# Feed-forward of a two-block transformer kernel: the order of a chunk's send and the fetch of the chunk before it

## The reference

```python
def swiglu(h, w_gu, w_down):
    gate, up = jnp.split(h @ w_gu, 2, axis=-1)
    return (jax.nn.silu(gate) * up) @ w_down

for i in range(DEPTH):                                   # 4
    x = x + 0.5 * swiglu(rmsnorm(x, ffn1_norm[i]), ffn1_w_gu[i], ffn1_w_down[i])
    ...                                                  # mixer of layer i
    x = x + 0.5 * swiglu(rmsnorm(x, ffn2_norm[i]), ffn2_w_gu[i], ffn2_w_down[i])
```

## Time and profile before

| | |
|---|---|
| median of three runs | 2867.24 us (2863.96 to 2867.93) |
| profiled execution | 2865.28 us, of which the span is 2863.5 us |
| TensorE busy in the span | 2830.5 us, 99% |
| VectorE, ScalarE, GpSimd busy | 69%, 57%, 16% |
| DMA, mean over the span | 212 GB/s |

### The profile page before, as it was taken

The page is one execution under the profiler, slowest core; times in us unless marked ns, Lnnn a source line. Parts: engine busy times, 40 slices in busy tenths (PEclk is TensorE's granted clock), DMA queues, the critical chain, the costliest instruction groups (busy, mean ns, idle before and its releaser), DMA issues. The chain is left out here.

```text
span 2863.5 us, 36218 instructions
## 1 busy us (share of the span) xinstructions
PE 2830.5 (99%) x14207; PEld 2400.4 (84%) x14207; DVE 1966.8 (69%) x2300; ACT 1636.1 (57%) x2030; POOL 444.8 (16%) x724
## 2 busy tenths in 40 slices
PE   9999999999999999999999999999999999999998
PEld 7889888888988888888888898878888888888887
DVE  6868578677667768567767686676675765665764
ACT  5547755555464555565555487654566563566562
POOL 0304412021002112041201116111000020000020
PEclk9999999999999999999999999999999999999999
DMA  8964279697559779537869753596645696645694
GB/s 265 304 201 142 87 215 297 208 275 242 177 155 273 242 230 292 190 130 238 278 211 290 216 159 104 166 282 220 203 148 176 216 287 215 190 154 177 215 284 148
DMA packets 430842, 608.48 MB, mean 212 GB/s; under 512 B 21040, under 2 KB 282416, under 8 KB 430672
## 3 DMA queue, kind: packets, MB, share of 16 engines
q1 hardware_dynamic: 406416, 542.18, 60.1%
q0 software_dynamic: 23680, 62.95, 7.2%
q10 hardware_dynamic: 576, 1.05, 0.1%
HBM read 573.58 MB, written 32.51 MB: 212 GB/s over the span
## 5 line engine op out<-in xcount | busy, mean ns | idle before, releaser
L824 ACT ACTIVATE hi<-raw 128x2048 fp32r<-128x2048 f32 (+2 forms) x511 | 950.1, 1870 | 684.1 <-DMA raw<-in_ffn_w_gu 210.1
L862 DVE TENSOR_TENSOR lo<-raw,hi 128x2048 fp32r<-128x2048 f32 (+2 forms) x497 | 1098.3, 2229 | 277.8 <-ACT hi L824 276.2
L476 PE MATMUL ps<-hi,xh 128*128 128x512 f32 (+1 forms) x1952 | 766.9, 393 | 1.0 <-DVE lo L862 1.0
L478 PE MATMUL ps<-hi,xl 128*128 128x512 f32 (+1 forms) x1952 | 759.6, 389 | 0.0
L477 PE MATMUL ps<-lo,xh 128*128 128x512 f32 (+1 forms) x1952 | 759.0, 389 | 0.0
L478 PEld LDWEIGHTS ps<-hi,xl 128*128 128x128 f32 x1952 | 367.1, 188 | 76.0
L476 PEld LDWEIGHTS ps<-hi,xh 128*128 128x128 f32 x1952 | 367.5, 188 | 74.9 <-DVE lo L862 1.4
L477 PEld LDWEIGHTS ps<-lo,xh 128*128 128x128 f32 x1952 | 367.4, 188 | 72.7
L476 PE MATMUL ps<-hi,hhh 128*128 128x512 f32 x704 | 274.9, 390 | 0.6 <-DVE hhb L1352 0.6
L477 PE MATMUL ps<-lo,hhh 128*128 128x512 f32 x704 | 274.0, 389 | 0.0
L478 PE MATMUL ps<-hi,hhl 128*128 128x512 f32 x704 | 274.0, 389 | 0.0
(11 more groups left out here) (466 smaller groups left out, 3876.3 us busy)
## 6 DMA issues: line engine op xcount, KB each, us to landing
raw<-in_ffn_w_gu SPq DMA_DIRECT2D x396, 512.0 KB, 5.2
raw<-in_ffn_w_down SPq DMA_DIRECT2D x80, 1024.0 KB, 5.7
raw<-in_w_ff SPq DMA_DIRECT2D x64, 1024.0 KB, 5.6
raw<-in_w_in SPq DMA_DIRECT2D x60, 1024.0 KB, 5.3
raw<-in_gdn_w_in SPq DMA_DIRECT2D x32, 1024.0 KB, 5.6
turned<-hhf POOLq DMA_DIRECT2D x88, 256.0 KB, 4.5
hhr<-turned POOLq DMA_DIRECT2D x352, 64.0 KB, 4.2
raw<-in_sb_w_in SPq DMA_DIRECT2D x12, 1024.0 KB, 5.1
```

Of the source, the lines that this page charges most:

```text
L476: e.matmul(o, a1, r1, start=kk == 0, stop=False)
L478: i = e.matmul(o, a2, r1, start=False, stop=kk == kts - 1)
L824: k.e.activation(plan.part(m.hi, m, q), plan.part(m.raw, m, q), ACT.Copy).then_inc(*k.up("act_piece_hi", ("hi", q)))
L862: k.e.tensor_tensor(plan.part(m.lo, m, q), plan.part(m.raw, m, q), plan.part(m.hi, m, q).bitcast(F32), ALU.subtract).then_inc(*k.up("dve_p ...
```

## The change

`pool_hidden` is cut into two helpers, `send` and `fetch`, with the same instructions and waits as before. In the eight feed-forwards of the first block the order is the old one up to chunk 6. From chunk 7 on, chunk c is sent ahead of the fetch of chunk c - 1: send 7, send 8, fetch 7, send 9, fetch 8, send 10, fetch 9, fetch 10. The feed-forward of the second block (`ff2`) keeps the old order throughout.

```diff
     n = f.n // 4
-    for c in range(f.chunks):
+
+    def send(c):
         k.wait_ge("flip", g, c)
         if c >= 4:
             k.wait_ge("fetched", g, c - 4)
         k.e.dma_start(k.t["turned"][c % 4, :, 0:f.n], f.flipped[c % f.turns][:, :]).then_inc(*k.up(f"dma_send{c % 3}", ("sent", g, c), by=16))
+
+    def fetch(c):
         k.wait_ge("sent", g, c)
         for b in range(4):
             rows = k.t["turned"][c % 4, :, n * b:n * b + n].rearrange("(a i) r -> i a r", a=4)
             k.e.dma_start(f.raw[32 * b:32 * b + 32, c + 1, :].rearrange("i (a r) -> i a r", a=4), rows).then_inc(
                 *k.up(f"dma_fetch{c % 3}", *([("fetched", g, c)] if b == 3 else []), by=16))
+
+    ahead = 7 if si.name != "ff2" else f.chunks
+    for c in range(f.chunks):
+        send(c)
+        if c < ahead:
+            fetch(c)
+        elif c > ahead:
+            fetch(c - 1)
+    if ahead < f.chunks:
+        fetch(f.chunks - 1)
```

## The result

The changed kernel takes 2877.4 us (median of five runs, 2870.46 to 2881.11) against 2867.24 (five runs, 2863.45 to 2869.8). The ratio is 1.0032 with a 95% interval of 1.0019 to 1.0045: slower by about 9 us, with an interval of 5.4 to 12.9 us, where 1.4 were forecast. A second set of runs of the same kernel gave 1.0033 (1.0020 to 1.0045).

A forecast was written before the change was run, and what follows sets the result against it. TensorE, busy 2830.5 of 2863.5 us, was taken to bound the kernel. In the first feed-forward 1.5 + 6.9 - 7.0 = 1.4 us of stall, added to the median 2867.24, gave 2868.6 us; range 2865.0 to 2873.5.

The forecast's parts named there:

- the delay d: First feed-forward: how much later the fetch of 7 lands for ScalarE's turn; taken as 1.5 us, ends -0.4 and 4.4.
- The weight piece: First feed-forward, third piece of the down projection, behind the turn of 7: cover 2.26 us, so no cost at d 1.5.
- d - 2.26: TensorE's cost in us at that weight piece: nothing at d 1.5, 1.2 at 3.4.
- The term of the sum, chunk 9: First feed-forward: the fetch of 9 waits for flip 10 and the send of 10, stalling TensorE at chunk 10 by 1.4 us.
- d + L - 7.0: TensorE's stall at chunk 10 where positive; L, landing of the fetch of 9, taken as 6.9 us, between 3.85 and 8.65.
- The other seven: Later feed-forwards: cost taken as 0; second and fourth could pay up to 1.1 us each for the fetch of 9.
- Neither sign of being wrong: Wrong if TensorE idles over a microsecond in several other stretches, or flip 10 in the first does not follow turn 7.
- The slower one: Rival: fetch of 9 in the first feed-forward meets weight transfers, stall 5.1 to 6.0 us, 2872.3 to 2875.4 us; chance 0.13.
- The lower end of the range: Whole kernel at 2865.0 us: no cost, and what was called the lower run of the three before.

The follow-up runs named there:

- first_fetch9_late: Kernel before, with only send 9, send 10, fetch 9, fetch 10 of the new order, in the first feed-forward alone: median 2868.78 us, ratio 1.0008.
- first_fetch7_late: Kernel before, with only the fetch of 7 moved behind the send of 8, in the first feed-forward alone: median 2875.78 us, ratio 1.0033.
- others_only: Kernel before, with the new order in the seven later feed-forwards and the old one in the first: median 2867.22 us, ratio 1.0007.
- first_turn7_behind: Kernel before, new order in the first feed-forward alone, ScalarE's turn of 7 moved behind chunk 10's silu and three weight pieces: 2868.0 us, ratio 1.0006.

## Why the prediction was wrong

Two steps failed: the delay d was taken too small, and the path at chunk 10 was the wrong one, as its own round trip was left out. A third loss, the clock's, was in no term.

**The delay d of the turn of 7 (the size that failed).** The place and the chain were right: fetch of 7 at 127.9 (127.74), silus, weight piece and flip 10 all moved by d. The size was not. I took 1.5 us, because in the trace of before a later DMA landed nearly with an earlier one. It was 2.8 us here, and the turn started at 135.57, 136.59, 136.67 and 135.82 in the four other traces with a late fetch of 7, so d was 2.8 to 4.5, around the upper end that I had set at 3.4 to 4.4. (With the old order the turn itself started between 130.99 and 132.84 in four traces, so one or two microseconds of this can be scatter.) From its first issue to the turn the fetch took 7.3 to 8.6 us in the five, against 7.72 before: it did not catch up, and the turn moved by about as much as the issue had. Landing times of the four fetch DMAs of 7, and of those of 10, in the changed kernel (to lay beside the earlier trace rows):

```profile
DMA to landing us min/median/max: 2.4/2.9/5.6
DMA to landing us min/median/max: 4.3/4.5/5.1
```

Most of the four are quicker than before, but the turn waits for the last, and that took 5.6; in the four other traces the slowest took 6.0 to 7.0. The median of a group told nothing of its last member. An estimate from the fit in the Trainium skill ("DMA: Bandwidth & Descriptors", section "Anatomy of one DMA — SWDGE (gpsimd) path"), 2.15 us for 64 KB, is near the quickest DMA here (2.4) and far from the ones that count.

**The weight piece.** "d - 2.26" held. On TensorE's scale d is 2.8 + 0.27 (its down projection starts 0.27 us earlier here), which gives 0.8; the stop was 0.71 and in the other traces, with their larger d, 1.4 to 2.6. It was priced at nothing only because of d.

**The term of the sum, chunk 9 (the path that failed).** This was the wrong term, and putting the measured d into it does not mend the sum. Its rule d + L - 7.0 with the measured 3.07 and 5.6 (147.81 to 153.40) gives 1.7, close to the 1.4 forecast, and the chain it describes did end when it said: the turn of 9, the weight piece at 154.72, done at 157.0. TensorE read chunk 10 only at 160.40. What it waited for was the turn of 10, which started at 159.56, held up by its own data. I had written that chunk 10 is ready then "even if its own rows came early" and never asked when they come. Flip 10 was 2.8 us late; GpSimd waited for its send, issued at 147.26, until 152.62, 5.4 us where it had been 3.0 before (144.46 to 147.44); the fetch took 6.2 us to ScalarE's 158.84, where it had been 4.9 (147.44 to 152.37). These three make 6.5 us. The rows of the kernel before for this step, from the timelines of GpSimd, ScalarE and VectorE:

```profile
147.44 0.56 POOL L1216 DMA_DIRECT2D hhr<-turned  x1 [2.42 <-DMA turned<-hhf]
```

```profile
152.37 0.63 ACT L1224 ACTIVATE hhh<-hhr 128x512 fp32r<-128x512 f32 x1 [4.04 <-DMA hhr<-turned]
```

```profile
153.09 0.69 DVE L1235 TENSOR_TENSOR hhl<-hhr,hhh 128x512 fp32r<-128x512 f32 x1 [1.78 <-ACT hhh L1224]
```

Chunk 10 was whole at 153.78 there and TensorE read it at 156.33: a cover of 2.55 us. A delay of 6.5 us uses it up, and even d = 1.5 would have, with a trip as slow as this. The send of 10 took 5.2 to 5.4 us in four of the five late traces; in the fifth, the second of the changed kernel, it took 3.1, TensorE was already late by its earlier stop, and there was none at chunk 10. In `first_fetch9_late` the fetch of 9 behind flip 10 cost TensorE nothing, and `first_fetch7_late` has the whole loss without it. So that the sum had a stop at chunk 10 at all was luck.

**The granted clock.** No term of the sum and no rival had it: 1.7 us after the stop. The prediction asked only what the clock could give (1.00 in all its windows), not what a stop might take.

**The other seven.** Nearly right: taken at 0, with up to 1.1 each for the second and fourth. These two stopped for 0.73 and 0.45 us in the trace, where none was forecast, and in the timing `others_only` is level with the kernel against itself. No gain showed either, as the table of windows had said. Neither sign of being wrong came: no other stretch gained a microsecond of idle time, and flip 10 did move with the turn of 7. The signs watched the steps that held.

**The rivals.** The slower one had the sign and, in its price of 2872.3 to 2875.4, the size of several of these runs, but it rested on the fetch of 9 meeting the weights, and `first_fetch7_late` has the loss with that fetch early. Its true form had all its parts in the text: the silus and weight pieces behind the turn of 7, flip 10 behind them. I gave d a value between its ends where the nearest evidence, the last DMA's 6.1 us in the earlier trace rows, lay at the upper one. The lower end of the range, 2865.0, is also not the lowest of the three runs, which was 2863.96.

What stays open is why the last of the four DMAs took some 3 us longer than the others, and why the send of 10 took 5.4 us instead of 3.0. Weight transfers run in the same stretch, but no experiment held them back.

## What to carry to other kernels

Before moving a transfer on one queue, ask what stands in order behind the instruction that waits for it, on the engine where it waits: here a turn that could start 5.5 us later without a cost that showed (137.72 against 132.19) held up a weight piece with 2.3 us of cover and a flip on which the last round trip hung. Price a set of DMAs by the last that lands, and price the moved chunk's own way to the end as well as its neighbour's. If an operation that waits isn't needed soon, try it behind those that are: here that made the new order of the transfers harmless.

## What the runs showed of the hardware

A stop of TensorE was mostly followed by a further loss. In four of the five traces with a late fetch of 7 the granted clock went to half after a stop of 2.1 to 3.4 us (at 162 to 165 us in the rows above, at 142 in the second trace of the changed kernel); in the fifth, with stops of 2.6 and 3.0, it stayed at 1.00 in this stretch. In the seven traces without such a stop it was 1.00 in the same stretch. In the first trace of the changed kernel the half clock cost 1.7 us on top of the 4.3 up to chunk 10. That the stop made the clock fall is argued from these traces and not shown: the clock also fell where TensorE had no such stop, in a mixer of the kernel before (0.66 from 281 to 286 us, no wait over 0.8 us in 272 to 292), and in the trace of `first_turn7_behind` it stood at 1.00 from 270 to 300.

The clock goes with the scatter of the runs. Of the 75 runs of the kernel before beside these experiments, the 16 at a mean granted clock of 0.999 took 2864.9 us on average, the 41 at 0.998 took 2866.9, the 16 at 0.997 took 2868.1 and the two at 0.996 took 2874.7.
